# Second mixer, pairs 1 to 6: the next pair's projections directly behind a step's scores

## The reference, cut to what matters

```python
q, k, v = b_project(x, pos, w_qkv, b_qkv)         # x @ w_qkv + b_qkv, partial rotary on q and k
qb = q.reshape(B, nb, BLOCK_B, N_KV_HEADS_B, GQA_B, HEAD_DIM)
kk = band_pair(k...)                               # previous block of 128 keys, then the current one
vv = band_pair(v...)
s = jnp.einsum('bnqhgd,bnphd->bhgnqp', qb, kk).astype(jnp.float32) * SCALE
mask = (dist >= 0) & (dist < WINDOW_B) & ((blk > 0) | (p >= BLOCK_B))
probs = sink_softmax(s, mask, sinks)               # max, exp, sum and the sink's exp, division
o = jnp.einsum('bhgnqp,bnphd->bnqhgd', probs, vv)
return o @ w_o + b_o, ...
```

## Time and profile before

| | us |
|---|---|
| median of three runs | 3235.17 |
| profiled execution | 3240.25 |
| its span | 3238.5 |
| PE (TensorE matmuls) busy | 3118.2 (96%) |
| DVE (VectorE) busy | 1736.0 (54%) |
| ACT (ScalarE) busy | 1591.4 (49%) |
| POOL (GpSimd) busy | 1704.6 (53%) |

### The profile page before, as it was taken

How to read it: one execution, slowest core, us unless ns; L and a number is a source line. 1 busy time by engine, 2 the same in 40 slices (tenths; PEclk the granted TensorE clock), 3 DMA queues, 4 the chain that set the end, 5 groups by cost and what they waited for, 6 DMA issues and landing times. The chain is left out here.

```text
span 3238.5 us, 56473 instructions
## 1 busy us (share of the span) xinstructions
PE 3118.2 (96%) x21556; PEld 3040.4 (94%) x21556; DVE 1736.0 (54%) x3645; ACT 1591.4 (49%) x3330; POOL 1704.6 (53%) x1420
## 2 busy tenths in 40 slices
PE   8999999999999969999999999989899999999997
PEld 7999999999999949999999999988789999999997
DVE  4445555454555536665363365389856653433653
ACT  4555555555555514454353354367644543533542
POOL 5555555555555505665465475454246654554653
PEclk9999999999999979999999999999999999999998
DMA  5665676666667375443444444321153444444442
GB/s 211 247 237 201 240 252 217 235 246 246 223 236 271 107 272 192 131 142 122 139 132 142 140 135 151 114 62 40 41 192 131 132 134 137 151 138 135 162 151 95
DMA packets 134909, 540.93 MB, mean 167 GB/s; under 512 B 24880, under 2 KB 49248, under 8 KB 131808
## 3 DMA queue, kind: packets, MB, share of 16 engines
q1 hardware_dynamic: 133440, 536.51, 49.0%
q10 hardware_dynamic: 784, 0.60, 0.1%
q0 software_dynamic: 416, 0.21, 0.0%
HBM read 497.53 MB, written 216.90 MB: 221 GB/s over the span
## 5 line engine op out<-in xcount | busy, mean ns | idle before, releaser
L1289 ACT CAST w_hi<-raw 128x1024 fp32r<-128x1024 f32 (+1 forms) x459 | 471.4, 1027 | 844.0 <-PE bank L103 797.3
L1488 DVE TENSOR_TENSOR w_lo<-raw,w_hi 128x1024 fp32r<-128x1024 f32 (+1 forms) x229 | 327.3, 1429 | 731.7 <-ACT w_hi L1289 731.7
L101 PE MATMUL bank<-x_hi,w_hi 128*128 128x352 f32 (+1 forms) x2208 | 712.1, 322 | 5.7 <-POOL w_lo L1407 4.4
L102 PE MATMUL bank<-x_lo,w_hi 128*128 128x352 f32 (+1 forms) x2208 | 705.9, 320 | 0.0
L103 PE MATMUL bank<-x_hi,w_lo 128*128 128x352 f32 (+1 forms) x2208 | 702.5, 318 | 0.0
L1407 POOL TENSOR_TENSOR w_lo<-raw,w_hi 128x1024 fp32r<-128x1024 f32 (+1 forms) x230 | 547.8, 2382 | 280.4 <-ACT w_hi L1289 280.4
L101 PE MATMUL a_gemm<-x_hi,a_w_hi 128*128 128x352 f32 (+1 forms) x1728 | 560.6, 324 | 11.2 <-DVE x_lo L636 11.1
L102 PE MATMUL a_gemm<-x_lo,a_w_hi 128*128 128x352 f32 (+1 forms) x1728 | 553.4, 320 | 0.0
L103 PE MATMUL a_gemm<-x_hi,a_w_lo 128*128 128x352 f32 (+1 forms) x1728 | 551.4, 319 | 0.0
L101 PE MATMUL bank<-t_h_hi,w_hi 128*128 128x352 f32 (+1 forms) x1440 | 465.4, 323 | 11.2 <-POOL t_h_lo L1427 6.2
L103 PE MATMUL bank<-t_h_hi,w_lo 128*128 128x352 f32 (+1 forms) x1440 | 464.5, 323 | 0.0
(11 more groups left out here) (291 smaller groups left out, 5538.8 us busy)
## 6 DMA issues: line engine op xcount, KB each, us to landing
raw<-w_up SPq DMA_DIRECT2D x264, 512.0 KB, 3.7
roll<-cache SPq DMA_DIRECT2D x128, 1023.5 KB
raw<-w_down SPq DMA_DIRECT2D x96, 512.0 KB, 3.6
a_raw<-w_a SPq DMA_DIRECT2D x72, 512.0 KB, 5.1
roll<-cache SPq DMA_DIRECT2D x16, 2044.0 KB
raw<-w_o SPq DMA_DIRECT2D x48, 512.0 KB, 3.7
raw<-w_down SPq DMA_DIRECT2D x48, 384.0 KB, 3.2
vT<-a_vt SPq DMA_DIRECT2D x24, 516.0 KB, 7.7
```

The costliest lines, as they stand in the source:

```text
L101: pe.matmul(out, w_hi, x_hi, start=first, stop=False)
L102: pe.matmul(out, w_hi, x_lo, start=False, stop=False)
L1289: act.copy(w_hi[:, b % RING, cols], raw[:, b % RING, cols]).then_inc(s_whi, 1)
L1488: dve.tensor_tensor(w_lo[:, b % RING, cols], raw[:, b % RING, cols], f32(w_hi[:, b % RING, cols]), ALU.subtract).then_inc(s_wlo[1], 1)
```

## The change

A function `filled(s)` is true for the steps 4 to 27 (pairs 1 to 6). In these

- TensorE issues `part` directly behind `scores`, where it stood behind `weigh_values`;
- ScalarE issues `high_probs(s-2)` last in its body, behind exponentials, weight split and `evacuate`, and `evacuate_o` one body later, at its head;
- VectorE issues `low_probs(s-2)` behind `rotate`, where it stood ahead of it.

The first pair and the last steps keep their order. GpSimd and SyncE are not touched, and no instruction is added or removed.

```diff
+        def filled(s):
+            return PER <= s < NSTEP - PER
...
@@ ScalarE
             def body(s):
                 n, j = divmod(s, PER)
-                if 0 <= s - 2 < NSTEP:
+                if filled(s - 1):
+                    evacuate_o(s - 4)
+                if 0 <= s - 2 < NSTEP and not filled(s):
                     high_probs(s - 2)
-                if 0 <= s - 3:
+                if 0 <= s - 3 and not filled(s):
                     evacuate_o(s - 3)
...
                 if projected(s) is not None:
                     evacuate(projected(s) + 3)
+                if filled(s):
+                    high_probs(s - 2)
...
@@ VectorE
                 if 0 <= s - 1 < NSTEP:
                     invert(s - 1)
-                if 0 <= s - 2 < NSTEP:
+                if 0 <= s - 2 < NSTEP and not filled(s):
                     low_probs(s - 2)
                 if rotated(s) is not None:
                     rotate(rotated(s))
+                if filled(s):
+                    low_probs(s - 2)
...
@@ TensorE
                 if s < NSTEP:
                     scores(s)
+                if filled(s):
+                    part(*divmod(s, PER))
                 if 0 <= s - 2 < NSTEP:
                     transpose_probs(s - 2)
                 if 0 <= s - 3:
                     weigh_values(s - 3)
-                if s // PER + 1 < PAIRS:
+                if s < PER:
                     part(*divmod(s, PER))
```

## The result

The changed kernel is slower. Twelve runs beside twelve of the kernel before gave medians of 3245.1 and 3238.13 us; the ratio is 1.0020, 95% interval 1.0011 to 1.0029, so 3.6 to 9.4 us more. The forecast was 3233.3 us, in a range up to 3243. The time is 2.1 us outside it, and on the other side of the kernel before. The range was counted from the three-run median of 3235.17, and twelve runs put the kernel before at 3238.13: on the forecast's own base the ratio gives 3241.6, inside the range. The direction is wrong on either base.

The account below looks back on a forecast made before the run. TensorE and VectorE both nearly full, a VectorE-ScalarE loop taking over: pairs 25.50 + 100.56 + 24.21, sum 150.3 against 152.1 us, exit even. The 1.9 us gain from the 3235.17 median gave 3233.3 us, range 3227 to 3243.

Parts of the forecast that it names:

- TensorE's holds at the first scores: TensorE's waits between scores and transposes, about 1.6 us per pair with the other steps; all were to go.
- the loop: Chain of VectorE and ScalarE without TensorE, forecast to take over at 25.14 us per pair; TensorE alone would need 24.2.
- j=1: Second step of a pair, with the weight split; forecast 7.25 us.
- j=2: Third step of a pair, low halves one block shorter; forecast 5.83 us, the split over 0.4 before the minimum.
- j=0: First step of a pair; forecast 5.99 us, a small operation after the minimum held by GpSimd's cosine product.
- VectorE's 2.3 us of blocks behind the split: Two small VectorE operations per pair standing behind GpSimd operations, 1.61 + 0.71 us; forecast to go.
- The gap in j=3: Fourth step of a pair: the minimum gets through between GpSimd's q low part and cosine product; 6.07 us, chance 0.42.
- the rival: Fourth step's minimum is held for the cosine product: 3.1 us slower, 3238.3; chance 0.28, with or without the first step.
- The exit: Step 28, in the old order: taken as even, bounds one hold of 0.97 us either way.
- The last rival: Minimum of the third step also held behind the cosine product after a late split: 3244 us; chance 0.17 including unseen stalls.
- the second case: Fourth step's minimum held for the cosine product, 5.0 us in six pairs: 3238.3; chance 0.28, with or without the first step.
- The rule on the port: Whichever of VectorE and GpSimd issues first holds the shared port pair throughout; shared bandwidth would be about 1 us per pair shorter.

Follow-up runs that it names:

- e3: Changed kernel with GpSimd issuing the cosine product ahead of q's low part in steps 4 to 27; ratio 0.9991 to the kernel before, 24.46 us per pair.
- e1: Changed kernel with 18 additional TensorE matmuls, result unused, between scores and transposes of step 28; ratio 1.0006 to the kernel before.
- e5: Changed kernel with the edits of e3 and e4 together; ratio 0.9974 to the kernel before, 24.34 us per pair.
- e4: Changed kernel, second step's weight split moved: ScalarE copies ahead of the exponentials, VectorE subtracts instead of GpSimd; ratio 0.9998 to the kernel before, 24.87 us per pair.
- e6: Kernel before with only GpSimd's cosine product put ahead of q's low part in steps 4 to 27; ratio 1.0005 to the kernel before, 25.99 us per pair.
- e2: Changed kernel with the new order in pairs 1 to 5 only, pair 6 in the old order; ratio 1.0016 to the kernel before.

## Why the prediction was wrong

- **What bounds, and the loop.** Right. TensorE's holds at the first scores went, and the loop masks, minimum, exponentials, eviction, high halves, low halves took over. Step by step: j=1 7.20 us (forecast 7.25), j=2 5.84 (5.83), j=0 5.84 (5.90 with the gap missed, 5.99 hit). VectorE's 2.3 us of blocks behind the split went.
- **The gap in j=3.** "I take the gap as hit in j=3" failed. The coin fell on the other side: j=3 took 6.92 (6.07 with the gap hit, 6.99 with it missed). This alone turned the sign of the pairs, from 1.9 us won to 2.2 lost. (The prediction calls j=2's margin of 0.4 eight times that of j=3; by its own sums, 7.32 and 7.34, j=3's is 0.02.) The pairs came out at 25.80, between the 25.14 of my forecast and the 25.97 of the rival. Pair 1 took 26.30 and pair 6 24.88, the rival's 26.33 and 25.04 within 0.2. Masks 4 to 28 were 154.37 us apart and the rival's sum was 155.3. So this rival was right, at 2.2 us more in place of 3.1. e3 shows that the gap is the cause: with the order of the two products turned, j=3 took 6.14.
- **The exit.** This step failed too, and it is the larger one: "The exit (step 28, in the old order) I take as even ... bounds are one hold of 0.97 either way." The runs showed 4.92 us and a hold of 3.27, not 0.97. I had written that TensorE runs ahead, that its transposes are issued 4 us before they are wanted, and that this feeds nothing back. It doesn't as long as projections fill the lead. In step 28 there are none, so the whole lead becomes one hold, and the clock falls in it. With that hold filled (e1) or the lead gone (e5) the exit is back at 17.11. I read the granted clock only where it was 1.00, though it is 0.87 in the kernel before over 2310 to 2348, where it falls from 2331 on, behind the exit: close by, this kernel does lose clock to waits. The prediction has no price for that anywhere.
- **The sum.** From the forecast's 150.3 to the measured 154.37 it is 4.1 us in the pairs, and 4.9 in the exit: 9.0. The forecast was 1.9 us won and the medians say 7.0 lost, 8.9 apart; with an interval of 3 us either way, so near an agreement is luck. The prediction also took under 0.2% as not to be told from no change; twelve runs of each gave an interval of 0.09% either way.
- **The range.** The last rival, all three places lost, would have given 3244, near the measured time, but not for that reason: the minimum of j=2 ran free. The time came from the second case and an exit that no case had.
- **The rule on the port.** The page "SBUF — State Buffer" of the Trainium skill says, in "Who interferes with whom", that the operation that issues first keeps the shared pair for its whole length. It says this of VectorE's modes that use both port pairs; of an operation with two inputs in SBUF, as the minimum is, it says that it contends with a GpSimd operation that reads SBUF. The minimum at 2230.20 stood until the cosine product of 2230.18 ended: the trace agrees, and this alone made j=3 0.8 us longer (e3).

## What to carry to other kernels

When work is moved so that an engine gets ahead, look where the lead is given back: there it stands in one piece, and TensorE can pay for that with its clock too (4.9 us here for a hold of 3.3). A bubble is only removed if the next bound is lower; otherwise first shorten the chain that takes over (here the edits of e3 and e4, together 0.3% under the kernel before). And where VectorE's small operations open a chain, order GpSimd's operations so that the last one, not the first, ends when they are issued; e6 shows that this is worth nothing where another block in the same loop takes its place.

## What the runs showed of the hardware

- A hold of 3.3 to 3.5 us, on a TensorE that was busy throughout before, was followed by the half clock in all three kernels with one: in the changed kernel and in e2 from within the hold (value products 1.59 us behind the transposes' start for 0.98), in e4 from a good microsecond behind it. In e1 the same hold filled with matmuls left the clock at 1.00. In the kernel before, holds of 0.97 left it at 1.00.
- A hold of 2.35 us, before the scores of step 29, left the clock at 1.00 in the kernel before, in e1 and in e5, and was followed by the half clock in e2 and e6, all five with no hold over 0.2 us ahead of it in step 28. What decides between the two, no run here shows.
- A hold of 1.87 us in step 28 of e3 was followed by full speed at once (value products 0.98 behind the transposes' start) and half clock in step 29 (1.62), behind the 2.36 us hold there. By e2 and e6 that second hold can do it by itself; whether the first had a part stays open.
- Of two GpSimd operations back to back, a VectorE operation that arrives within 0.02 us of the change stands behind the second. It did so in all six pairs of the changed kernel (0.93 to 0.96 us each), so this is no jitter.
